# A new order for the opening of a three-layer transformer kernel, and pooling units taken last

## The reference

```
m  = silu(cond) @ ada_w + ada_b            # 6 x 1024 values, for c and for c_ctx
h  = rmsnorm(x) * g * (1 + scale) + shift  # shift = m[0:1024], scale = m[1024:2048]
a, q, k, v = split(h @ w_in)               # 256 pooling, 768 q, 256 k, 256 v columns
q, k = rope(rmsnorm per head)
attn = softmax(q k^T / 8) v                # x over ctx and x, ctx over ctx
pool = einsum(window_mean(a) - a, w_grp) * ch_scale   # windows 2, 4, 8, 16
x += gate * (concat(pool, attn) @ w_out)   # then a gated feed-forward layer
```

## Time and profile before

| | us |
|---|---|
| median of 3 runs | 2540.08 (2538.51 to 2540.66) |
| the profiled execution, its own time | 2537.89 |
| its span in the profile | 2536.1 |
| mean granted TensorE clock, of full speed | 0.981 |
| TensorE busy | 2442.1 (96%) |
| VectorE, ScalarE, POOL busy | 996.0, 851.0, 772.9 |
| first product of a column unit starts | 56.28 |
| first scores of the attention start | 214.22 |
| first output product starts | 368.69 |

### The profile page before, as it was taken

How to read it: one execution, slowest core, us unless ns; L and a number is a source line. 1 busy time by engine, 2 the same in 40 slices (tenths; PEclk the granted TensorE clock), 3 DMA queues, 4 the chain that set the end, 5 groups by cost and what they waited for, 6 DMA issues and landing times.

```text
span 2536.1 us, 34037 instructions
## 1 busy us (share of the span) xinstructions
PE 2442.1 (96%) x13345; PEld 1915.0 (76%) x13345; DVE 996.0 (39%) x1426; ACT 851.0 (34%) x1382; POOL 772.9 (30%) x413
## 2 busy tenths in 40 slices
PE   6998999999999999999899999999999998999998
PEld 3676667788888888688577768888887656888887
DVE  4356651411122112544456332221527665523322
ACT  3224652322122122332556332222423564322321
POOL 1161001223232323231011234444543531444443
PEclk8999999999999999999999999999999998999999
DMA  7540006521222223422020243333333200333332
GB/s 262 166 108 26 1 1 214 168 67 58 67 58 66 62 61 94 127 67 52 7 43 10 59 133 100 96 94 100 91 100 83 81 1 26 92 98 93 100 98 76
DMA packets 335970, 209.76 MB, mean 83 GB/s; under 512 B 29299, under 2 KB 308444, under 8 KB 335842
## 3 DMA queue, kind: packets, MB, share of 16 engines
q1 hardware_dynamic: 332880, 201.89, 27.2%
q10 hardware_dynamic: 2898, 6.05, 0.7%
q0 software_dynamic: 64, 0.04, 0.0%
HBM read 205.82 MB, written 2.12 MB: 82 GB/s over the span
## 4 chain that ended last, share of the span: by engine, by line
PE 84%; issue 5%; DVE 5%; DMA 2%; ACT 2%; POOL 2%; SPq 0%; DVEq 0%; ACTq 0%; POOLq 0%
PE G L1579 21%; PE G L1580 21%; PE G L1581 21%; PE G L1775 5%; PE G L1803 4%; PE G L1788 4%; DMA raw<-in_l_ada_w_dram 2%; POOL wlo L898 2%; PE G L1650 1%; PE G L1746 1%; PE G L1617 1%; PE G L1821 1%; PE G L1601 1%; DVE ssq L2046 1%; PE G L1602 1%
## 5 line engine op out<-in xcount | busy, mean ns | idle before, releaser
L898 POOL TENSOR_TENSOR wlo<-raw,whi 128x1024 fp32r<-128x1024 f32 x282 | 680.1, 2412 | 1528.8 <-ACT whi L1084 1528.7
L1579 PE MATMUL G<-big_a,whi 128*128 128x512 f32 x2016 | 743.7, 369 | 8.5 <-POOL wlo L898 4.9
L1580 PE MATMUL G<-big_a,wlo 128*128 128x512 f32 x2016 | 729.3, 362 | 0.0
L1084 ACT ACTIVATE whi<-raw 128x1024 fp32r<-128x1024 f32 x282 | 298.9, 1060 | 1275.7 <-PE G L1581 1127.5
L1581 PE MATMUL G<-big_a,whi 128*128 128x512 f32 x2016 | 726.0, 360 | 0.0
L1579 PEld LDWEIGHTS G<-big_a,whi 128*128 128x128 f32 x2016 | 380.9, 189 | 86.5 <-issue 15.1
L1580 PEld LDWEIGHTS G<-big_a,wlo 128*128 128x128 f32 x2016 | 380.7, 189 | 63.8 <-issue 7.0
L1581 PEld LDWEIGHTS G<-big_a,whi 128*128 128x128 f32 x2016 | 379.5, 188 | 60.5
L1579 PE MATMUL G<-big_b,whi 128*128 128x512 f32 x856 | 315.7, 369 | 3.2 <-POOL wlo L898 2.3
L1580 PE MATMUL G<-big_b,wlo 128*128 128x512 f32 x856 | 315.6, 369 | 0.0
L1581 PE MATMUL G<-big_b,whi 128*128 128x512 f32 x856 | 314.3, 367 | 0.0
(11 more groups left out here) (245 smaller groups left out, 2277.7 us busy)
## 6 DMA issues: line engine op xcount, KB each, us to landing
raw<-in_l_ada_w_dram SPq DMA_DIRECT2D x96, 512.0 KB, 5.0
raw<-in_l_ffn_w_gate_dram SPq DMA_DIRECT2D x44, 512.0 KB, 3.8
raw<-in_l_ffn_w_up_dram SPq DMA_DIRECT2D x44, 512.0 KB, 3.8
raw<-in_l_ffn_w_down_dram SPq DMA_DIRECT2D x32, 512.0 KB, 4.0
raw<-in_w_up_dram SPq DMA_DIRECT2D x32, 512.0 KB, 4.0
raw<-in_w_down_dram SPq DMA_DIRECT2D x32, 512.0 KB, 3.7
raw<-in_w_in_dram SPq DMA_DIRECT2D x28, 512.0 KB, 3.8
raw<-in_l_w_in_dram SPq DMA_DIRECT2D x24, 512.0 KB, 3.9
```

The costliest lines, as they stand in the source:

```text
L898: pool.tensor_tensor(wlo[:, u % 2], raw[:, r % RING], whi[:, u % 2].bitcast(F32), ALU.subtract).then_inc(raw_free[r % RING], 1)
L1084: act.activation(whi[:, u % 2], raw[:, r % RING], ACT.Copy).then_inc(hi_done, 1)
L1579: pe.matmul(o, whi[:, u % 2, k], rlo[:, k, t0:t0 + w], start=k == 0, stop=False)
L1580: pe.matmul(o, wlo[:, u % 2, k], rhi[:, k, t0:t0 + w], start=False, stop=False)
```

## The change

Groups 1, 2 and 3 no longer go through the ring. Each has places of its own in regions that are free in the opening (`staged`), so that SP issues them without waiting. The small vectors move from ScalarE's queue to SP's, between groups 1 and 2; the rope table, the counts and the pooling weights move behind the norm on ScalarE's queue. The sum of squares is now taken over the untransposed tokens by ScalarE (six passes of 1024 columns that write their sum), and no longer by squares of the turned tiles. VectorE copies four of the turned tiles and ScalarE the other four. The root is spread as before, but VectorE multiplies the tokens by it (`xn`) before the factors are known. The scale factors come in halves: group 2 gives the gain of input tiles 0 to 3, group 3 that of tiles 4 to 7. Group 3 is multiplied and turned inside `first_units`, after the second and the third input tile. ScalarE and VectorE now form the high part and the full value each from `xn`. POOL's `lower` of units 0 and 1 goes in four quarters.

The units of `in0` are in the order keys (0, 1), queries (2 to 7), values (8, 9), pooling (10, 11). Modulation groups 4 to 9 stand behind units 2 to 7, where they stood behind units 0 to 5. POOL does all its window work after the last `lower` of this stage, and TensorE's pooling product comes behind the attention. The first output unit takes its input tiles in the order 2 to 7, 0, 1, and waits for the pooled tiles ahead of 0 and 1.

The diff, cut:

```diff
+        def staged(i, q):
+            if i == 3:
+                return part(bf if q < 2 else af, (6144 if q < 2 else 10240) + 1024 * (q % 2), 2, 512)
+            return part(af, 6144 + 1024 * q, 2, 512) if i == 1 else part(bf, 8192 + 1024 * q, 2, 512)
...
-        XIN_AFTER = ((0, 1), (2, 3, 4), (5, 6, 7), ())
-        for i in range(4):
-            plan_ada(0, i)
-            plan_aux(("adaT", 0, i - 1) if i else "vec")
-            for m in XIN_AFTER[i]:
-                plan_aux(("xin", m))
-        plan_aux(("adaT", 0, 3))
+        plan_ada(0, 0)
+        for m in range(4):
+            plan_aux(("xin", m))
+        for i in (1, 2):
+            for q in range(4):
+                plan["ada", 0, i, q] = (None, None, cnt["g"])
+            cnt["g"] += 1
+            if i == 1:
+                for m in range(4, KD):
+                    plan_aux(("xin", m))
+                plan_aux(("spread", 0))
+                plan_aux("vec")
+                plan_aux(("adaT", 0, 0))
+        plan_aux(("adaT", 0, 1))
+        plan_aux(("adaT", 0, 2))
...
-        S0, L0_Q, L0_POOL, L0_V = {}, range(4, 10), (2, 3), (10, 11)
+        S0, L0_Q, L0_V, L0_POOL = {}, range(2, 8), (8, 9), (10, 11)
...
-        ADA_IN0 = [(0, 4 + i) for i in range(6)]
+        LAST_GAIN = (0, 3)
+        ADA_IN0 = [LAST_GAIN, None] + [(0, 4 + i) for i in range(6)]
...
 SP, after group 0:
-                sp.dma_start(mats[:, 1:6], A["mats"][:, 1:6]).then_inc(PH["set", "mats"], 16)
+                sp.dma_start(ones_d, A["mats"][:, 1]).then_inc(PH["set", "ones"], 16)
+                for q in range(4):
+                    load_staged(1, q)
+                ... the 24 small vectors ...
+                for q in range(4):
+                    load_staged(2, q)
...
-            for i in range(1, 4):
-                ada(0, i)
...
+                    if st == "in0" and n == 1:
+                        for q in range(4):
+                            load_staged(3, q)
+                        sp.dma_start(mats[:, 2:6], A["mats"][:, 2:6]).then_inc(PH["set", "mats"], 16)
...
 POOL:
+                for k in range(0, KD, 2 if u < 2 else KD):
+                    ks = slice(k, k + (2 if u < 2 else KD))
+                    ins = pool.tensor_tensor(wlo[:, u % 2, ks], raw[:, r % RING, ks], whi[:, u % 2, ks].bitcast(F32),
+                                             ALU.subtract)
...
             for u in range(0, first["wout", 0, 0] + 2):
                 lower(u)
-                if u == 6:
...
+            pool.wait_ge(*when(("set", "icnt"), 16))
+            pool.wait_ge(*when(("in0", "rotated"), 8))
+            for i in range(2):
+                key = ("in0", "U", L0_POOL[i])
+                pool.wait_ge(gfree[group_of(key) % 4], group_of(key) // 4 + 1)
+                window_sums(i)
+                if i:
+                    wider_sums()
+                window_means(i, 0)
+                window_means(i, 1)
+                pool.sem_inc(PH["in0", "pooled"], 1)
...
 ScalarE:
+            act.wait_ge(*when(("set", "padrow"), 32))
+            act.wait_ge(*when(("set", "xload"), 16))
+            for t in range(6):
+                if t == 4:
+                    act.wait_ge(*when(("set", "cload"), 16))
+                ins = act.activation(bf[:, D * t:D * t + D], xtok[:, t, :], ACT.Square, accum_out=stat[:, 2, t:t + 1])
+            ins.then_inc(PH["set", "rest"], 1)
+            act.wait_ge(*when(("set", "rest"), 1))
+            act.activation(rsb[:, 1, 0:6], stat[:, 2, 0:6], ACT.Sqrt, bias=eps[:, 0:1],
+                           scale=1.0 / D).then_inc(PH["norm0", "std"], 1)
+            ada(0, 0)
+            ada(0, 1)
+            for m in range(4, KD):
+                ... xT[:, m] <- ps(("xin", m)) ...
+            act.wait_ge(*auxiliary("vec"))
+            act.dma_start(halves[0:12], A["mats"][0:12, 6]).then_inc(PH["set", "halves"], 16)
+            ada(0, 2)
+            upper(0)
+            upper(1)
+            def first_norm(k):
+                act.wait_ge(*when(("set", "xnorm"), k + 1))
+                for q, (t0, w) in enumerate(X_CTX):
+                    ins = act.activation(hhi[:, k, t0:t0 + w], xn[:, k, t0:t0 + w], ACT.Identity,
+                                         bias=mod[:, 0, k, q:q + 1], scale=amix[:, 0, k, q:q + 1])
+                ins.then_inc(PH["norm0", "hi"], 1)
+            act.wait_ge(*when(("set", "gain"), 1))
+            for k in range(4):
+                first_norm(k)
+            ada(*LAST_GAIN)
+            act.wait_ge(*when(("set", "gain"), 2))
+            for k in range(4, KD):
+                first_norm(k)
...
 TensorE:
+            ada(0, 0)
+            ... waits for xload and cload ...
+            for m in range(4):
+                turn_tokens(m)
+            ada_staged(1)
+            for m in range(4, KD):
+                turn_tokens(m)
+            ... spread of the root, turn of the vectors ...
+            ada_turn(0, 0)
+            ada_staged(2)
+            ada_turn(0, 1)
+            ada_turn(0, 2)
             inputs("in0", S0, L0_V, (hhi, hlo), 12, lambda n: X_CTX, h_ready=("norm0", "h"))
-            pe.wait_ge(*when(("in0", "pooled"), 1))
+            pe.wait_ge(*when(("in0", "rotated"), 8))
+            pe.wait_ge(*when(("in0", "vdone"), 2))
+            all_groups(IN0_END)
+            pair_attention()
+            pe.wait_ge(*when(("in0", "pooled"), 2))
             pe.wait_ge(*when(("set", "poolw"), 64))
             ... the two pooling products ...
-            pe.wait_ge(*when(("in0", "rotated"), 8))
-            pe.wait_ge(*when(("in0", "vdone"), 2))
-            all_groups(group_of(("pool", 1)) + 1)
-            pair_attention()
...
+                            late = {1: lambda: ada_staged(3), 2: lambda: ada_turn(*LAST_GAIN)} if st == "in0" else {}
+                            first_units([(st, "U", 0), (st, "U", 1)], ranges_of, h_ready, between=late)
...
+                square(("wout", l), rhs, ranges, ada_groups=ADA_WOUT0, first_order=(2, 3, 4, 5, 6, 7, 0, 1),
+                       between={7: pooled_tiles})
...
 VectorE:
+            for m in range(KD):
+                if m >= 4:
+                    dve.wait_ge(*when(("set", "xact"), m - 3))
+                dve.tensor_tensor(xn[:, m, :], xT[:, m, :], ps(key), ALU.mult).then_inc(PH["set", "xnorm"], 1)
...
+            def first_norm(k0):
+                for k in range(k0, k0 + 4):
+                    if k >= 2:
+                        dve.wait_ge(*when(("norm0", "h"), k - 1))
+                    for q, (t0, w) in enumerate(X_CTX):
+                        ins = dve.tensor_scalar(tmp[:, k % 2, t0:t0 + w], xn[:, k, t0:t0 + w], amix[:, 0, k, q:q + 1],
+                                                mod[:, 0, k, q:q + 1], ALU.mult, ALU.add)
+                    ins.then_inc(PH["norm0", "tmp"], 1)
+                    dve.wait_ge(*when(("norm0", "tmp"), k + 1))
+                    dve.wait_ge(*when(("norm0", "hi"), k + 1))
+                    dve.tensor_tensor(hlo[:, k, :], tmp[:, k % 2, :], hhi[:, k, :].bitcast(F32),
+                                      ALU.subtract).then_inc(PH["norm0", "h"], 1)
+            first_gain(2)
+            first_norm(0)
+            first_gain(3)
+            first_norm(4)
```

More of the change, by code:

```diff
@@ L777, in inputs @@
                         ada(*hosted[n])
[L778 removed]
+                    if st == "in0" and n == 1:
+                        for q in range(4):
+                            load_staged(3, q)
+                        sp.dma_start(mats[:, 2:6], A["mats"][:, 2:6]).then_inc(PH["set", "mats"], 16)
+                    if n < len(ada_groups) and ada_groups[n] not in (None, LAST_GAIN):
                         load(plan[st, "U", n + 1][1], [(w[:, :, c:c + m], m) for c, m in cols[n + 1]])
@@ L1566, in take_group, with unit @@
                     pe.wait_ge(gfree[g % 4], g // 4)
-            def unit(key, rhi, rlo, ranges, k_tiles=KD, j=0, h_ready=None, between={}):
+            def unit(key, rhi, rlo, ranges, k_tiles=KD, j=0, h_ready=None, between={}, order=None):
                 u, r, g = plan[key]
@@ L1573, in unit @@
                     pe.wait_ge(gfree[g % 4], g // 4 + j)
-                for k in range(k_tiles):
+                order = order or tuple(range(k_tiles))
+                for k in order:
                     if h_ready is not None:
@@ L1585, in unit, with first_units @@
                         between[k]()
-            def first_units(keys, ranges_of, h_ready, rhs=(hhi, hlo), order=range(KD), after=0):
+            def first_units(keys, ranges_of, h_ready, rhs=(hhi, hlo), order=range(KD), after=0, between={}):
                 for key in keys:
@@ L1605, in first_units @@
                         mm.then_inc(unit_done, 1)
+                    if i == len(keys) - 1 and at in between:
+                        between[at]()
             def ada(l, i):
@@ L1619, in ada, with ada_staged @@
                     mm.then_inc(raw_free[r % RING], 1)
+            def ada_staged(i):
```

(31 more changed lines are left out.)

231 lines of the change are left out of this document (110 added, 121 removed).

## The result

The changed kernel takes **2511.92 us** (median of 4 runs, 2510.99 to 2513.43) against 2540.37 in the same session (2538.51 to 2540.70): ratio 0.989, 95% interval 0.9873 to 0.9907, 28.5 us faster. A second session gave 2511.24 against 2541.52 (0.9889, 0.987 to 0.9908). The forecast was 2510.5. The profiled execution took 2511.91, its span is 2510.1.

The account below looks back on a forecast made before the run. TensorE is busy 96% of the span, so only idle and low-clock stretches can be won: -11.4 - 7.4 - 7.3 - 2.9 - 0.7 = -29.7 us on 2537.89, 2508.2; median 2510.5, 8 in 10 2504 to 2524.

Parts of the forecast that it names:

- First product: Opening, up to the first column unit's start: first product at 41.8 us instead of 56.28, VectorE's eight multiplications the longest piece.
- Loads: Opening loads: group 1 lands near 21.5 us, group 2 near 27.5, both units' weights near 30, group 3 near 36.
- Rival A: Opening bound by more than counted, late loads or low clock: first product near 50, +8 us, 2518; chance 0.15.
- First two units: First two column units of the input products: both end at 64.5 us against 75.89, -11.4 us.
- Unit 2: Third column unit: starts at 67.7 us instead of 91.20; with groups 4 and 5 added to the steady part, -7.4.
- rival B: Gaps move to unit 3 or the groups behind unit 2 on the four-slot ring: +9 us, 2519; chance 0.10.
- Before the attention: Between last input product and attention: 1.3 us of waiting instead of 8.62, -7.3 us, as pool units come last.
- The attention: Attention's first microseconds: clock stays up, so 5.84 busy us at 0.50 become 2.9, -2.9; POOL's work beside it costs 0.
- Rival C: In the attention, POOL's 27 us hold VectorE as a whole: -2.7 us in all, 2537; chance 0.03.
- rival D: VectorE's attention work starves POOL, so TensorE waits for pooled tiles behind it: 2583 at 10 us per instruction; chance 0.03.
- Behind the attention: Pool products fill 2.09 idle us (+0.9) and the clock stays up in the first output product (-1.6): -0.7 us.
- its last 2157 us are copied: After layer 0's first output product nothing is changed, so the remaining 2157 us were taken over as they were.

Follow-up runs that it names:

- xn_twice: Changed kernel with each of VectorE's eight multiplications of tokens by spread factors done twice; first product 8.0 us later, median 5.8 to 6.5 us above the changed kernel's two.
- whole_lower: Changed kernel with POOL making the low halves of units 0 and 1 in one instruction each, not quarters; first product at 41.29 us.
- split_vectors: Changed kernel plus early turns of groups 1 and 2, multiplications 5 to 8 after first normalised tiles, vectors on ScalarE's queue; first product 4.8 us earlier, median not distinguishable.

## Why the prediction was right

**First product, 41.8 forecast, 41.55 measured**, by errors that cancel. ScalarE's squares ended at 20.1 and freed the accumulator in time, so the fourth token tile did not wait (four tiles in 2.88, no gap), and the spread was there at 27.98 instead of 29.8. The multiplications came one per 0.875 us, not 0.95: done at 34.98, not 37.5. But from there to the first scaling it took 4.05 us, not 2.1: I had two turns and columns, and left out VectorE's copies of the vectors, the second turn's 1.54, and a gain held by POOL. Scaling to product took 2.5, not 2.2, and ScalarE's high half, not the scaling I reckoned with, is what the subtraction waited for (39.03 to 40.34).

**Loads.** Group 2 was forecast at 27.5. SP's timeline shows why it came later:

```profile
4.86 8.44 SPq L756 DMA_DIRECT2D plain_a<-in_l_ada_w_dram  x4
...
21.24 1.92 SPq L756 DMA_DIRECT2D plain_b<-in_l_ada_w_dram  x4
```

Group 1 waits for no slot, as intended, but its four issues waited on the queue and held SP for 8.44 us. The 24 vectors followed, and group 2 was issued only at 21.24; from 21.5 to 24.5 the DMA engines moved 208 GB/s, where it had been 372 to 393. TensorE waited for its last piece until 31.2. The forecast gave 10 us of slack before VectorE's end, it was 3.8, and nothing was lost. Rival A (loads bind the opening) is excluded by xn_twice.

**First two units, 64.5 forecast, 64.48 measured.** The granted 0.90 cost 2.3 us of 22.93 (2.7 taken) and pauses 0.7; the other 20 are full-rate work (16.8, 1.9 and 0.8 forecast). The scaling pair took 0.86, not 0.65. -11.4 stands.

**Unit 2, 67.7 and 67.80; last unit, 186.8 and 186.39.** The groups moved into the steady part cost 4.2 (118.59 less 114.40), forecast 4.7: TensorE's work grew by 5.2, and 1.0 of it took the place of pauses. No gap before unit 3 or 4: rival B is excluded.

**Before the attention**, 1.12 us (1.3 forecast). **The attention**, 149.41 us from first score to the pooling products, 152.38 before: -2.97, forecast -2.9. Rival C said POOL would hold VectorE. Windows of VectorE over the whole attention, before and after, show otherwise:

```profile
214.20:366.60 152.40, 144.56 (x1278) 97.48 (x1278) 94.17 (x237) 95.08 (x214) 0.00 (x0) 0.97 0.01 1
```

```profile
187.50:336.90 149.40, 141.57 (x1278) 96.30 (x1278) 94.06 (x237) 97.11 (x216) 27.71 (x23) 1.00 0.02 5
```

237 VectorE instructions take 94.17 us alone and 94.06 beside 27.71 us of POOL. Nor did POOL suffer: window work from 190.63 to 217.8, 27.2 us, no instruction above 1.86, ready 119 us before it is wanted (rival D excluded, at this size).

The forecast misread its own row here. The instruction of 1.89 us in the earlier trace rows (L2134) ends at 165.18, 0.55 us after POOL's at 164.63, not with it; and the PSUM row of 0.68 ends at 162.66, before that POOL row starts. It did run beside the POOL instruction before that, which the rows leave out (line 1024, 161.32 to 162.66). The conclusion stands, on the attention's windows.

The rule of the Trainium skill that the forecast drew on ("SBUF — State Buffer", section "Who interferes with whom") agrees with them: VectorE's attention work, which reads PSUM, isn't held. The gain, with two inputs in SBUF, and the scaling, with one, were held by 0.6 and 0.4 us at 38 to 40; for the scaling the rule wants a two-port mode, and no view names the mode. The quarters, which I credited with limiting this, caused most of it, and made the first product 0.3 us later at most (41.55 against 41.29 in whole_lower).

**Behind the attention**: pooling products 2.50 in place of 2.09 idle, the first output unit 8.74 instead of 10.13: -0.98, forecast -0.7.

**The sum** at the end of the first output unit (378.82, now 348.16) is -30.7; forecast -29.7. The term that failed is the one I did not price: "its last 2157 us are copied". They were 2161.9 in this profile. In two sessions the medians fell by 28.5 and 30.3, so the forecast holds on them, while the two single profiles are 26.0 apart. How much of the 4.6 to 4.7 us belongs to the change and how much to the two executions is open.

## What to carry to other kernels

Judge a change by an instant in the trace just behind it, and the unchanged rest by itself: here the same instructions varied by 6 us, more than any refinement was worth. A delay of the first product does not cost its full length, nor does an advance give it, when TensorE would begin at the low clock or has other work to fit in: 4.8 us of delay cost nothing, 3.5 us of advance gave 1.3. Two edits can be one: pooling units last without their products behind the attention cost 37 us.

## What I had not expected of the hardware

- Four issues of 512 KB on SP's queue took 1.92 us with room ahead (21.24), and 8.44 us behind some 5 MB issued before them (4.86); everything behind them on the queue, small vectors too, comes that much later. Windows of the changed kernel while the vectors are on their way, and of split_vectors, where group 2 follows at once:

```profile
21.50:24.50 3.00, 3.00 (x26) 1.34 (x25) 2.56 (x4) 0.57 (x1) 0.00 (x0) 1.00 0.85 208
```

```profile
21.50:24.50 3.00, 3.00 (x28) 1.50 (x26) 2.71 (x3) 2.97 (x8) 0.00 (x0) 1.00 1.06 388
```

- The low clock can come 1.1 us after work has begun again, not with the pause before it, and after the same pause it need not come (above, in six of 13 profiles). The windows of the changed kernel, behind the second attention, where TensorE was idle for 0.89 us and started the output products at 1386.46:

```profile
1384.00:1387.60 3.60, 2.71 (x17) 1.53 (x14) 1.53 (x3) 0.63 (x1) 0.00 (x0) 1.00 0.02 5
1387.60:1391.30 3.70, 3.70 (x11) 2.89 (x10) 0.14 (x1) 0.00 (x0) 0.00 (x0) 0.54 0.00 0
1391.30:1395.00 3.70, 3.70 (x17) 3.02 (x17) 0.00 (x0) 0.00 (x0) 0.00 (x0) 1.00 0.00 0
```
